# NSA probability x value products in 64-column halves, one unit per head and branch; three PSUM banks for scores, two for turned probabilities, one for outputs

## The reference

```python
h = rms_norm(x, norm1); proj = h @ w_in
# differential attention: 4 heads, two 64-wide softmaxes each, values 128 wide
a = softmax(q0 k0 + bias) - lam * softmax(q1 k1 + bias);  o_diff = a @ v
# NSA: 8 heads, 64 wide, keys and values shared by groups of 4
o = g0 * (p_cmp @ v_cmp) + g1 * (p_slc @ v_slc) + g2 * (p_win @ v_win)
x = x + concat(rms(o_diff), rms(o_nsa)) @ w_out
x = x + (silu(h2 @ w_gate) * (h2 @ w_up)) @ w_down;  return rms_norm(x)
```

## Time and profile before

| what | us |
|---|---|
| median of 3 runs (650.07 to 651.05) | 651.03 |
| the profiled execution | 652.01 |
| its span, first to last instruction | 650.2 |
| mean granted TensorE clock | 0.999 |
| busy in the span: TensorE products | 638.5 |
| busy: weight loads | 571.1 |
| busy: VectorE, ScalarE, GpSimd | 452.8, 354.5, 245.5 |

### The profile page before, as it was taken

One profiled execution on the slowest core, in us unless ns is written; L12 is line 12 of the kernel. 1 busy time (PEld: TensorE's weight loads), 2 busy tenths in 40 slices (PEclk: granted clock), 3 DMA queues, 4 the chain that ended last, 5 costly groups with the idle time before them and its releaser, 6 DMA issues.

```text
span 650.2 us, 11350 instructions
## 1 busy us (share of the span) xinstructions
PE 638.5 (98%) x4029; PEld 571.1 (88%) x4029; DVE 452.8 (70%) x957; ACT 354.5 (55%) x697; POOL 245.5 (38%) x152
## 2 busy tenths in 40 slices
PE   8999999999999999999999999999999999999996
PEld 7888998988899887888888899999999998888884
DVE  5435437655656887634279898888988898788984
ACT  7646435879565568625332464444454456655653
POOL 4766344575161542453302103435353320121521
PEclk9999999999999999999999999999999999999999
DMA  8979979479997998997399957878777668989813
GB/s 245 274 177 232 256 201 230 109 196 329 278 233 174 228 203 217 188 229 206 111 305 283 257 162 245 256 231 253 219 241 216 198 219 318 318 243 257 291 64 129
DMA packets 116007, 146.58 MB, mean 225 GB/s; under 512 B 5252, under 2 KB 73968, under 8 KB 115952
## 3 DMA queue, kind: packets, MB, share of 16 engines
q1 hardware_dynamic: 96936, 110.49, 53.9%
q0 software_dynamic: 16352, 30.84, 27.2%
q10 hardware_dynamic: 2664, 4.53, 2.0%
HBM read 139.53 MB, written 59.00 MB: 305 GB/s over the span
## 4 chain that ended last, share of the span: by engine, by line
PE 95%; DVE 2%; DMA 1%; issue 1%; POOL 1%; ACT 0%; DVEq 0%; ACTq 0%; POOLq 0%
PE bank L821 10%; PE bank L823 10%; PE bank L822 10%; PE bank L1161 8%; PE bank L1159 8%; PE bank L1160 8%; PE bank L840 7%; PE bank L842 7%; PE bank L841 7%; PE bank L1001 6%; PE bank L977 3%; PE bank L961 3%; PE bank L962 2%; PE bank L1040 1%; DMA rows<-in_cmp_pos_v_dram 1%
## 5 line engine op out<-in xcount | busy, mean ns | idle before, releaser
L766 POOL TENSOR_TENSOR w_lo<-raw,w_hi 128x1024 fp32r<-128x1024 f32 (+1 forms) x63 | 156.9, 2493 | 225.6 <-ACT w_hi L1202 224.7
L1202 ACT CAST w_hi<-raw 128x1024 fp32r<-128x1024 f32 (+2 forms) x123 | 127.1, 1039 | 123.2 <-PE bank L1161 44.9
L1676 DVE CUSTOM_DVE_ANT_0 bank<-bank,bias 128x128 f32<-128x128 f32 (+3 forms) x96 | 47.6, 497 | 75.8 <-PE bank L962 40.0
L1833 DVE TENSOR_TENSOR w_lo<-raw,w_hi 128x1024 fp32r<-128x1024 f32 (+1 forms) x61 | 72.9, 1195 | 12.9 <-ACT w_hi L1202 12.9
L840 PE MATMUL bank<-xT_hi,w_hi 128*128 128x512 f32 x200 | 79.9, 399 | 0.0
L842 PE MATMUL bank<-xT_hi,w_lo 128*128 128x512 f32 x200 | 78.7, 394 | 0.0
L841 PE MATMUL bank<-xT_lo,w_hi 128*128 128x512 f32 x200 | 78.6, 393 | 0.0
L1159 PE MATMUL bank<-xs,w_hi 128*128 128x256 f32 x256 | 72.3, 282 | 0.0
L1161 PE MATMUL bank<-xs,w_lo 128*128 128x256 f32 x256 | 72.2, 282 | 0.0
L1160 PE MATMUL bank<-xs,w_hi 128*128 128x256 f32 x256 | 72.2, 282 | 0.0
L787 POOL DMA_DIRECT2D down_sums<-in_w_down_dram x21 | 23.3, 1111 | 109.6 <-DMA down_sums<-in_w_down_dram 54.9
(11 more groups left out here) (287 smaller groups left out, 1703.8 us busy)
## 6 DMA issues: line engine op xcount, KB each, us to landing
raw<-mixed_sums SPq DMA_DIRECT2D x32, 512.0 KB, 4.8
raw<-in_w_gate_dram SPq DMA_DIRECT2D x22, 512.0 KB, 4.8
raw<-in_w_in_dram SPq DMA_DIRECT2D x20, 512.0 KB, 5.5
down_sums<-in_w_down_dram POOLq DMA_DIRECT2D x17, 512.0 KB, 8.7
mixed_sums<-in_w_up_dram SPq DMA_DIRECT2D x16, 512.0 KB, 10.8
mixed_sums<-in_w_gate_dram SPq DMA_DIRECT2D x16, 512.0 KB, 9.1
mixed_sums<-mixed_sums POOLq DMA_DIRECT2D x16, 512.0 KB, 12.6
raw<-in_w_up_dram SPq DMA_DIRECT2D x14, 512.0 KB, 4.8
```

Source lines behind the costliest of these rows:

```text
L766: nc.gpsimd.tensor_tensor(wv_lo(k)[:, 0:n], raw_at(k)[:, 0:n], wv_hi(k)[:, 0:n].bitcast(F32), ALU.subtract).then_inc(s_split, 1)
L1202: nc.scalar.copy(wv_hi(k)[:, 0:n], raw_at(k)[:, 0:n]).then_inc(s_whi, 1)
L1833: nc.vector.tensor_tensor(wv_lo(k)[:, 0:n], raw_at(k)[:, 0:n], wv_hi(k)[:, 0:n].bitcast(F32), ALU.subtract).then_inc(s_dlo, 1)
```

## The change

The 15 NSA groups before the last become *units*: the values of the four slots of a head and branch are issued together, after the last of the four is turned, each product as two, with 64 stationary columns each, that write partitions 0 to 63 and 64 to 127 of the output bank. The last group, diff and cmp slots stay one unit a slot, at full width. There is one output bank (`OUT`), so that `values` waits for the reading of the unit just before; the bank set free goes to scores, which now wait for slot s - 3. `gather` reads four tiles of a unit in a row. Turned probabilities are kept in `PT` (1024 columns) and in `sq` by a table of places, and `copy_turned` waits for the last unit that used its place. The jobs dq 3 and dk 3 change places, `lambda_products` writes into `lam_in`, and the clearing of `sq` goes. Core of the diff:

```diff
-             ("dq", 3), ("dk", 3), ("mt", 4), ("mt", 6), ("mt", 5)]
+             ("dk", 3), ("dq", 3), ("mt", 4), ("mt", 6), ("mt", 5)]
...
+    last_group = [s for s in range(last_nsa - NT + 1, last_nsa + 1)]
+    units = []
+    for s in turned:
+        if slots[s][0] != "nsa" or s in last_group:
+            units.append((s,))
+        elif slots[s][3] == NT - 1:
+            units.append(tuple(range(s - NT + 1, s + 1)))
+    unit_at = {u[-1]: n for n, u in enumerate(units)}
+    unit_of = {s: n for n, u in enumerate(units) for s in u}
+    of_upto = [sum(1 for u in units[:n + 1] if slots[u[0]][0] != "diff") for n in range(len(units))]
+    od_upto = [n + 1 - of_upto[n] for n in range(len(units))]
+    def place_of_probs(s):
+
+        kind, h, b, i = slots[s]
+        if kind == "cmp":
+            return 0, 6 * P, 2 * P
+        if kind == "diff":
+            return (0, 0, (i + 1) * P) if s > last_nsa and i % 2 == 0 else (1, 0, (i + 1) * P)
+        if i == NT - 1:
+            return 1, 0, NT * P
+        first = 6 * P if i == 0 and s < last_free and (s // NT) % 2 else (0, P, 3 * P)[i]
+        return 0, first, (i + 1) * P
+
+    def held_by(s):
+
+        which, lo, n = place_of_probs(s)
+        mine = [unit_of[x_] for x_ in range(s) if x_ in turn and place_of_probs(x_)[0] == which
+                and place_of_probs(x_)[1] < lo + n and lo < sum(place_of_probs(x_)[1:])]
+        return max(mine, default=None)
...
-        PROJ, SCORE, TURN, OUTP = ps[0:2], ps[2:4], ps[4:6], ps[6:8]
+        PROJ, SCORE, TURN, OUT = ps[0:2], [ps[2], ps[3], ps[6]], ps[4:6], ps[7]
...
-            PT = sb("PT", [P, 2, 512], F32, attention)
+            PT = sb("PT", [P, 1024], F32, attention)
...
             def scores(s):
                 kind, h, b, i = slots[s]
-                bank = SCORE[s % 2]
+                bank = SCORE[s % 3]
                 pe.wait_ge(s_evac, needed(slots[s], ("q", "k", "dq", "dk", "hc")))
                 if kind == "diff":
                     pe.wait_ge(s_dup[h], 32)
-                if s >= 2 and slots[s - 2][0] == "diff" and slots[s - 2][2] == 1:
-                    pe.wait_ge(s_comb, sum(1 for z in slots[:s - 1] if z[0] == "diff" and z[2] == 1))
-                elif s >= 2:
-                    pe.wait_ge(s_exp, s - 1)
+                if s >= 3 and slots[s - 3][0] == "diff" and slots[s - 3][2] == 1:
+                    pe.wait_ge(s_comb, sum(1 for z in slots[:s - 2] if z[0] == "diff" and z[2] == 1))
+                elif s >= 3:
+                    pe.wait_ge(s_exp, s - 2)
...
             def values(s):
-                if s not in turn:
+                if s not in unit_at:
                     return
-                kind, h, b, i = slots[s]
-                n = turn[s]
-                bank = OUTP[n % 2]
+                n = unit_at[s]
+                kind, h, b, _ = slots[s]
+                bank = OUT
                 pe.wait_ge(s_evac, needed(slots[s], ("dv",)))
-                pe.wait_ge(s_pt, n + 1)
-                if n >= 2 and slots[turned[n - 2]][0] == "diff":
-                    pe.wait_ge(s_odf, od_upto[n - 2])
-                elif n >= 2:
-                    pe.wait_ge(s_of, of_upto[n - 2])
+                pe.wait_ge(s_pt, turn[s] + 1)
+                if n >= 1 and slots[units[n - 1][0]][0] == "diff":
+                    pe.wait_ge(s_odf, od_upto[n - 1])
+                elif n >= 1:
+                    pe.wait_ge(s_of, of_upto[n - 1])
...
+                elif len(units[n]) > 1:
+
+                    for s_ in units[n]:
+                        i = slots[s_][3]
+                        for j in range(i + 1):
+                            v = v_nsa[:, b, j, g * HD:(g + 1) * HD]
+                            for half in (0, HD):
+                                mm = nc.tensor.matmul(bank[half:half + HD, i * HD:(i + 1) * HD],
+                                                      probs(s_)[:, j * P + half:j * P + half + HD], v,
+                                                      start=j == 0, stop=j == i)
...
-                if n >= 2:
-                    act.wait_ge(s_pv, n - 1)
-                nc.scalar.copy(PT[:, n % 2, 0:w], TURN[n % 2][:, 0:w]).then_inc(s_pt, 1)
+                if held_by(s) is not None:
+                    act.wait_ge(s_pv, held_by(s) + 1)
+                nc.scalar.copy(probs(s), TURN[n % 2][:, 0:w]).then_inc(s_pt, 1)
...
-                    ins = nc.vector.tensor_tensor_reduce(out=sq[:, n * HD:(n + 1) * HD], in0=lam_in[:, 2 * n, :],
+                    ins = nc.vector.tensor_tensor_reduce(out=lam_in[:, 2 * n, :], in0=lam_in[:, 2 * n, :],
...
+                    if b or h >= late_head:
                         dve.wait_ge(s_of, of_upto[n] - 1)
-                        nc.vector.scalar_tensor_tensor(out=m, in0=bank[:, 0:HD], scalar=coef[:, s:s + 1], in1=m,
-                                                       op0=ALU.mult, op1=ALU.add).then_inc(s_of, 1)
+                    for s_ in units[n]:
+                        i = slots[s_][3]
+                        m = mix[:, i, 512 + h * HD:512 + (h + 1) * HD]
+                        z = bank[:, i * HD:(i + 1) * HD] if len(units[n]) > 1 else bank[:, 0:HD]
+                        if b == 0 and h < late_head:
+                            ins = nc.vector.tensor_scalar(m, z, coef[:, s_:s_ + 1], None, ALU.mult)
+                        else:
+                            ins = nc.vector.scalar_tensor_tensor(out=m, in0=z, scalar=coef[:, s_:s_ + 1], in1=m,
+                                                                 op0=ALU.mult, op1=ALU.add)
+                    ins.then_inc(s_of, 1)
...
-            link(nc.vector.memset(sq[:, :], 0.0))
```

More of the change, by code:

```diff
@@ L288, in hymba_block @@
     last_diff_qk = {h: max(i for i, x_ in enumerate(slots) if x_[:2] == ("diff", h)) for h in range(DIFF_HEADS)}
+    last_free = min(i for i, x_ in enumerate(slots) if x_[0] == "diff")
     cmp_slot = [i for i, x_ in enumerate(slots) if x_[0] == "cmp"]
@@ L648, in low_done, with probs @@
             eng.wait_ge(s_dlo if by_dve[k] else s_split, sum(by_dve[m] == by_dve[k] for m in range(k + 1)))
-        SHARE = OUTP[(len(turned) - 1) % 2][:, 256:512]
+        SHARE = OUT[:, 256:512]
+        def probs(s):
+            which, lo, n = place_of_probs(s)
+            return (PT, sq)[which][:, lo:lo + n]
         def od_bank(dh, t):
@@ L876, in proj_piece @@
                     if a >= 4:
-                        pe.wait_ge(s_of, of_upto[turn[last_nsa if a == 7 else cmp_last]])
+                        pe.wait_ge(s_of, of_upto[unit_of[last_nsa if a == 7 else cmp_last]])
                     else:
@@ L997, in values @@
                 else:
-                    g = h // HEADS_PER_GROUP
+                    i = slots[s][3]
                     for j in range(i + 1):
                         v = v_nsa[:, b, j, g * HD:(g + 1) * HD] if kind == "nsa" else v_diff[:, j, h * P:(h + 1) * P]
-                        mm = nc.tensor.matmul(bank[:, 0:v.shape[1]], PT[:, n % 2, j * P:(j + 1) * P], v,
+                        mm = nc.tensor.matmul(bank[:, 0:v.shape[1]], probs(s)[:, j * P:(j + 1) * P], v,
                                               start=j == 0, stop=j == i)
@@ L1292, in copy_turned @@
                 act.wait_ge(s_turn, n + 1)
-                if n >= 2:
-                    act.wait_ge(s_pv, n - 1)
-                nc.scalar.copy(PT[:, n % 2, 0:w], TURN[n % 2][:, 0:w]).then_inc(s_pt, 1)
+                if held_by(s) is not None:
+                    act.wait_ge(s_pv, held_by(s) + 1)
+                nc.scalar.copy(probs(s), TURN[n % 2][:, 0:w]).then_inc(s_pt, 1)
             def gather_diff(s):
-                if s not in turn or slots[s][0] != "diff":
+                if s not in unit_at or slots[s][0] != "diff":
                     return
                 _, h, _, i = slots[s]
-                n = turn[s]
-                bank = OUTP[n % 2]
+                n = unit_at[s]
+                bank = OUT
                 act.wait_ge(s_pv, n + 1)
@@ L1378, in _ @@
                     t = slots[s - 6][3]
-                    act.wait_ge(s_of, of_upto[turn[s - 6]])
+                    act.wait_ge(s_of, of_upto[unit_of[s - 6]])
                     square(mix[:, t, 512:1024], mixT[:, 14 + t % 2, :], t, 4 + t)
@@ L1714, in gather @@
             def gather(s):
-                if s not in turn or slots[s][0] == "diff":
+                if s not in unit_at or slots[s][0] == "diff":
                     return
-                kind, h, b, i = slots[s]
-                n = turn[s]
-                bank = OUTP[n % 2]
+                kind, h, b, _ = slots[s]
+                n = unit_at[s]
+                bank = OUT
                 dve.wait_ge(s_pv, n + 1)
@@ L1723, in gather @@
                     dve.wait_ge(s_coefs, sum(1 for z in slots[:s] if z[0] == "nsa" and z[3] == NT - 1) + 1)
-                    m = mix[:, i, 512 + h * HD:512 + (h + 1) * HD]
-                    if b == 0 and h < late_head:
```

(8 more changed lines are left out.)

15 lines of the change are left out of this document (7 added, 8 removed).

## The result

The changed kernel takes 655.36 us (median of 4 runs, 654.23 to 657.0) where the kernel before takes 651.04: a ratio of 1.0072, 95% interval 1.0048 to 1.0095. It is slower; I had forecast 645.9 us and faster. The profiled execution took 655.39 us, its span 653.6.

A forecast was written before the change was run, and what follows sets the result against it. TensorE, busy 638.5 of 650.2 us, was taken to bound the kernel. The terms -12.6 + 4.5 + 3.5 + 1.0 - 1.5 = -5.1 us gave a median of 645.9 us, with a stated range of 638.5 to 662.

The forecast's parts named there:

- a new wait of TensorE costs its length: Attention, 40 to 276 us: TensorE busy 231.96 of 236 us at clock 1.00, so any wait added there lengthens the kernel equally.
- the list of new waits: TensorE's waits in attention: +3.5 us in the last group, +1.0 around cmp slots, -1.5 for scores.
- The value products: NSA value products before the last group: 600 half pairs at 0.034 us instead of 300 at 0.110, -12.6 us.
- The rival with halves in line: Value products: loads of two halves cannot overlap, +1.8 us instead of a gain; median 660.3 us, chance 0.34.
- The change of shape: Going in and out of the narrow array width once per unit: 15 x 2 x 0.15, +4.5 us.
- One output bank in the last group: Last group, one unit a step: values wait for VectorE's read of the slot before, +3.5 us, bounds 1.0 and 4.7.
- The cmp slots: Neighbouring units around the four cmp slots, whose outputs VectorE reads in eight instructions: +1.0 us for both places, bounds 0 and 3.
- Three score banks: Scores in attention: the three waits for the combination of the softmaxes go, -1.5 us, bounds -1.5 and 0.
- Moved work: Values of a unit's first three steps move to the fourth: TensorE's sum the same, VectorE and ScalarE catch up, no cost.
- The small edits: Dropping the clearing of sq (0.48 us of VectorE) and exchanging dq 3 and dk 3: nothing.
- the gain is there and eaten: Rival: halves at 0.040 us gain 9.0, waits and changes of shape take it back; +0.7, median 651.7 us, chance 0.12.

The follow-up runs named there:

- the idle products: Changed kernel with 6 idle products of ones ahead of the output-bank wait in each of the last group's four slots: 651.97 us.
- reading first: Changed kernel with VectorE reading outputs ahead of adding the bias: in the last group and the unit before it 650.12 us, in all steps 645.9 us.
- One side at a time: Changed kernel with each unit's halves reordered, all 10 products into partitions 0 to 63, then all 10 into 64 to 127: 668.11 us, single run.
- the banks alone: Kernel before with three banks for scores and one for outputs, no units, no halves: 697.22 us, ratio 1.0699.

## Why the prediction was wrong, step by step

*The step that failed: "a new wait of TensorE costs its length", and the list of new waits.* From slot 3 to slot 99 the changed kernel is 3.0 us longer: -10.2 of work, +8.7 of waiting, +4.5 of half clock. The prediction's terms for the same three were -8.1, +3.0 (3.5 + 1.0 - 1.5) and nothing. The work came out better than forecast; the waits were nearly three times as long, and the clock, which I had read as 1.00 in the earlier trace rows and taken for granted, was half for 10.2 us once TensorE waited 0.5 to 1.6 us again and again. That it follows on the waits is shown by the idle products and by reading first, both without half clock in this stretch.

*The value products: right, at the low end.* I took 0.034 us for a half between 0.029 and 0.058; it is 0.029, so the term is -15.6, not -12.6. One side at a time gave 0.057. The rival with halves in line falls. The Trainium skill's statement ("TensorEngine Tiling (Array Packing)", Tiling Modes) that tiles load and multiply in parallel agrees with the 0.029. The Trainium skill's stricter rule in "TensorE: Matmul & The Clock Gate" (The mechanism), that a load overlaps running products only if the row group differs, does not agree, as both halves have all rows.

*The change of shape: right.* 0.15 us and a little more each way in both traces; halves without units came out at +3.4 us where 64 such runs and the halves' spacing gave +3. With both terms, -15.6 + 4.5 = -11.1 for all 15 units, against 10.2 us less work measured.

*One output bank in the last group: too small.* I read waits of 1.8, 1.8 and 1.1 us off the trace and took 3.5 of at most 4.7. Four values wait 4.8 us; I had three, and had left out the first slot of the group. Its wait could be read off the trace too, as values and the read of the slot before them:

```profile
243.93 0.33 PE L1001 MATMUL bank<-v_nsa,PT 128*128 128x64 f32 x2
...
244.72 0.28 DVE L1729 SCALAR_TENSOR_TENSOR mix<-bank,coef,mix 128x64 f32<-128x64 f32 x1
```

In the changed kernel it waits for four reads in a row (1.63). From slot 87 to slot 92 the kernel loses 8.6 us. Idle time there is 6.2 us, against 1.0 before: the four waits and the 1.38 of the unit ahead of them. Some 0.6 is the unit's 40 half pairs where the kernel before has 8 whole ones. The rest, about 2.8, is the clock. I also took the waits as bare times, while each delays scores, hence the bias, hence the next read.

*The cmp slots: too small.* 1.0 us taken, bounds 0 and 3; TensorE waits 3.8 us for the output bank there. From slot 71 to 87 the lead falls by 2.2 us, although the gain of two units lies in it. Reading first in all steps is 4.2 us faster than in the last group alone.

*Three score banks: right in kind.* The waits for the combination are gone. With units and two score banks scores wait 6.8 us; with three, none. But 2.8 us come back as waits of a unit for ScalarE's copy.

*Moved work: wrong.* I put it at nothing, since the sum of TensorE's work is the same. In the changed kernel units wait 2.8 us for the copy of their fourth slot's turned probabilities. Units alone, without halves and with the old banks, cost 10 us; 3.9 of it is longer waiting, up to 3.4 half clock, and some 1.4 of busy time stays open. That the steps without values are too short for VectorE and ScalarE is my reading of the longer waits of scores; no run tests it by itself.

*The small edits: right*, as far as tried; the clearing of `sq` was not tried by itself.

The rival "the gain is there and eaten" was the nearest one: the right kind of loss at too small a price, 651.7 us with a chance of 0.12. It had no clock in it and halves at 0.040, so its own sum was off as well. The measured 655.4 lies inside the stated range of 638.5 to 662, but that range was wide for another reason, the halves in line; this is no credit to the forecast.

## What to carry to other kernels

A bank taken from double buffering is priced not by the length of the read, but by what the reader has ahead of it in its own queue, in every step in which the hand-over happens; moving the read to the front of the step turned a slower kernel (655.4) into the fastest (645.9). Where the bound engine gets new waits of a microsecond several times in a row, add the clock to the price: here 10.2 us at half clock cost 4.5, and in the kernel with the banks alone it was about half of the 46 us. A gain that was measured up to some slot is no gain of the kernel: follow the difference slot by slot to the end, and split it into busy and idle time of the bound engine. The difference of two kernels is not the worth of an edit as long as one of them spends more time at half clock.

## What the runs showed of the hardware that I had not expected

Products with 64 stationary columns that alternate between the two sides of the array are 0.029 us apart in plain float32 with 64 moving columns, load included, half of the 0.057 to 0.058 on one side. And the clock of an engine that is busy most of the time can fall in the middle of the kernel, though no single wait is longer than 1.8 us: in the kernel with the banks alone TensorE was busy 255.0 of 280 us, and the mean granted clock was 0.91. Whether it falls is not settled by the program alone: of two executions of one program, equally busy in the 15 us up to 220.9, one fell to 0.50 for 3.4 us and one did not.
